# A recurrent mixer reordered: gates between the halves of the output branch, sigmoids by tanh, POOL for squares and a series, the first weight tile in quarters

## The chip, the cores and the metric

One core of one Trainium2 chip runs the whole program in one launch. The metric is the device time in microseconds (us): the median of three runs was 1516.95 (1516.81 to 1517.58). The engines are named as in the profile: PE (matmuls, with PEld for its weight loads), DVE (vector), ACT (scalar functions), POOL (GpSimd) and SP (issues DMAs).

## The reference, cut to what matters

Four layers on x of 256 tokens by 1024 features, in float32. Each layer is a norm, a mixer, a residual sum, a norm, an MLP with squared ReLU and a residual sum. The mixers are a recurrent one (RG-LRU), a sparse attention, RWKV-7 and a differential attention. Only the first mixer, and what leads up to it, is changed:

```python
def _rmsnorm(x, g):
    return x * lax.rsqrt(jnp.mean(x * x, axis=-1, keepdims=True) + RMS_EPS) * g

def _rglru_mixer(h, w_in, conv_w, conv_b, w_a, b_a, w_x, b_x, lam, w_out):
    proj = h @ w_in                                   # 1024 x 2048
    y = jax.nn.gelu(proj[..., :D_RNN], approximate=True)
    xb = _causal_depthwise_conv(proj[..., D_RNN:], conv_w, conv_b)   # 4 taps
    xr = xb.reshape(B, S, RG_BLOCKS, RG_BLOCK_W)      # 4 blocks of 256
    r = jax.nn.sigmoid(jnp.einsum('bsnc,ncd->bsnd', xr, w_a).reshape(B, S, D_RNN) + b_a)
    i = jax.nn.sigmoid(jnp.einsum('bsnc,ncd->bsnd', xr, w_x).reshape(B, S, D_RNN) + b_x)
    log_a = -RG_C * r * jax.nn.softplus(-lam)         # RG_C = 8
    a = jnp.exp(log_a)
    u = jnp.sqrt(-jnp.expm1(2.0 * log_a)) * (i * xb)
    _, hs = lax.associative_scan(_lru_combine, (a, u), axis=1)
    return (hs * y) @ w_out
```

## The kernel before, in words

Everything stays in SBUF, features over the 128 partitions in 8 chunks of 256 tokens. The weights come in 96 tiles of 128 x 4096 floats (2 MB), in the order of `TILE_ORDER` (line 39), into a ring of three slots. SP issues the first DMAs at once (lines 386 to 394) and each later tile when PE is done with the tile three places before (`tile_done`, line 337).

A product is taken in three passes of reduced-width floats. So each weight tile is split in quarters of 1024 columns: ACT writes the high part (`split` in the scalar block, L1078), DVE the difference (`split` in the vector block, L1484), and PE multiplies high by high, high by low and low by high (`product`, L441 to L443). The activations are split in the same way. A projection (`project`, line 459) has four output chunks m, each of 8 k with 3 matmuls, 96 matmuls of 256 columns; two m fill one of the eight PSUM banks. It waits for each quarter only in its first m. The gate stage is 96 matmuls too, over four blocks, and waits for all four quarters of its tile before its first. The output projection (`project_out`) has two tiles of 96 matmuls with half tokens and 512 columns (L508 to L510).

The order on each engine is that of its block, written out by hand; a `wait_ge` on a semaphore holds all that stands behind it there. The banks are handed out in turn (`_turns`), and `open_bank` makes PE wait until what the bank held has been read.

The first mixer runs on PE as x0, tv (a small product for the last layer), x1, gates, y0, y1, o0, o1. ACT copies x0 and x1 out of PSUM (`conv_in`, L1170), DVE does the four taps of the convolution (one L1641 and three L1648 for each chunk), ACT and DVE split the result (`xc_high` L1174, `xc_low` L1655), ACT takes the sigmoids (L1196), then exp and tanh of the decay (L1203, L1204), DVE squares a and multiplies (L1673, L1675, and the input gate L1677), ACT takes the root (L1210), DVE multiplies (L1684) and scans (L1687), ACT takes the gelu of y (L1215, L1220), and h times y is formed and split (`hy` L1695, `values_high` L1157, `values_low` L1598). The softplus of lam is a series on 128 x 8 values on DVE (L1608 to L1636). In the first norm ACT squares (L1091) and takes the root (L1095), DVE applies it (L1527), PE transposes (L456), ACT and DVE split (L1101, L1540). POOL in this stretch only fetches rows of norm factors and stores tv; from 128 us on it does 16 multiplications for the second mixer (L2133).

Of the kernel before, what the change touches and what calls it, by code (L numbers as in the profile page):

```python
# [7 lines left out]
P = 128  # L8
D = 1024
# [25 lines left out]
def _mlp_tiles(layer):  # L35
# [4 lines left out]
    ["rg_x0", "rg_x1", "rg_gates", "rg_y0", "rg_y1", "rg_o0", "rg_o1"] + _mlp_tiles(0)  # L40
# [19 lines left out]
PARAM_COLS = [("conv_w", 32), ("conv_b", 8), ("b_a", 8), ("b_x", 8), ("lam", 8),  # L60
# [68 lines left out]
for _n, _w in [("rg_x0", 2), ("tv", 1), ("rg_x1", 2), ("rg_gates", 8), ("rg_y", 4)]:  # L129
    _turns(_n, _w)  # L130
# [31 lines left out]
for _u in range(12):  # L162
# [6 lines left out]
    if _u >= 5 and _u % 2 == 1:  # L169
# [5 lines left out]
TURN_OF = {"rg_x0": ("rg_x0", 1), "rg_x1": ("rg_x1", 1), "rg_gates": ("rg_gates", 7), "rg_y0": ("rg_y", 1),  # L175
# [9 lines left out]
def build(nc, weights, params, consts, rows, heads, t5, x_in, out):  # L185
# [8 lines left out]
    with ctx:  # L194
# [60 lines left out]
        SM_NLAM, SM_GSUB, SM_LAM, SM_BGATE, SM_SP = 560, 562, 564, 566, 568  # L255

# [125 lines left out]
        def _(sp):  # L382
# [3 lines left out]
            for th in range(2):  # L386
                sp.dma_start(x[:, th, :], x_in[:, th, :]).then_inc(x_loaded[th], 16)
            sp.dma_start(scales[:, 0, :], bass.AP(rows.tensor, 0, [[0, P], [1, D]])).then_inc(sig("first_row_in"), 16)
            sp.dma_start(con[:, :], consts).then_inc(sig("consts_in"), 16)
            load(0)  # L390
            sp.dma_start(par[:, :], params).then_inc(params_in, 16)
            load(1)
            sp.dma_start(t5_onehot, t5).then_inc(sig("t5_in"), 16)
            load(2)
            for n in range(RING, NTILES):
                tile_done(sp, TILE_ORDER[n - RING])
                load(n)
# [8 lines left out]
        def _(pe):  # L406
# [12 lines left out]
            def whole_tile(name):  # L419

                n = TILE_AT[name]
                pe.wait_ge(slot_full[n % RING], 16 * (n // RING + 1))
# [36 lines left out]
            def project(name, q, src, ready=None, warm=0, beside=None):  # L459

                w_hi, w_lo = split_tile(name)
                for m in range(4):
# [127 lines left out]
            pe.wait_ge(sig("consts_in"), 16)  # L590
            norm(0, 0)
            norm(0, 1)
            project("rg_x0", TURN["rg_x0"], act_split, lambda k: acts_in(0, k), warm=8)
# [7 lines left out]
            w_hi, w_lo = split_tile("rg_gates")  # L601
            for quarter in range(4):
                quarter_in("rg_gates", quarter)
            for blk in range(4):
                pe.wait_ge(sig("xc_split"), blk + 1)
                for g in range(2):
                    q = TURN["rg_gates"] + 2 * blk + g
                    open_bank(q)
                    for m in range(2):
# [450 lines left out]
        def _(act):  # L1060
# [42 lines left out]
            def norm(i, next_tile=None):  # L1103
# [10 lines left out]
                if i == 0:  # L1114
                    for th in range(2):
                        for n in range(2):
                            square(i, th, n)
# [1200 lines left out]
```

## Time and profile before

| | us |
|---|---|
| median of three runs | 1516.95 |
| profiled execution, its own time | 1518.57 |
| its span, first to last instruction | 1516.8 |
| PE busy | 1409.6 (93%) |
| DVE busy | 913.9 (60%) |
| ACT busy | 675.4 (45%) |
| POOL busy | 72.0 (5%) |
| mean granted TensorE clock | 0.972 |

The span is shared by four layers, and the stretch that the change touches is its first 130 us. What counts there is when PE may start the next product. The busy spans of matmuls overlap (each is modelled to its end), so the pace of PE is read from their start times.

### The profile page before, as it was taken

The numbers are of one execution on the slowest core, as the hardware profiler recorded it, in microseconds if no ns is written. First come the engines' busy times: TensorE is split into PE (matmuls) and PEld (weight loads), VectorE is DVE, ScalarE is ACT, GpSimd is POOL, SyncE is SP. The second block draws the span as 40 slices with busy tenths as digits, with TensorE's granted clock in tenths as the row PEclk, the third lists the DMA queues.
The fourth block names the chain that finished last, engine by engine and source line by source line (L and its number), as shares of the span: only waits on it lengthen the run. The fifth ranks groups of instructions, "written<-read, shape, count | busy, mean of one in ns | idle before, by whom it ended". The sixth has DMA issues, their size and how long they took to land.

```text
span 1516.8 us, 26931 instructions
## 1 busy us (share of the span) xinstructions
PE 1409.6 (93%) x11772; PEld 1233.9 (81%) x11782; DVE 913.9 (60%) x1448; ACT 675.4 (45%) x1145; POOL 72.0 (5%) x69
## 2 busy tenths in 40 slices
PE   6889999999789999999997987999999997899997
PEld 5877999988657899987897985799997974599996
DVE  6686555671485556555966434765557459855556
ACT  5844544552363445441821222354444445354452
POOL 0004000000141000000001310000000000000000
PEclk9989999999889999999999999999999999999999
DMA  7334554552301555453150000455545440245451
GB/s 306 138 123 155 197 192 175 207 183 87 142 1 56 182 189 200 167 192 130 67 189 37 4 3 30 158 190 177 212 167 190 173 166 1 102 160 210 167 195 55
DMA packets 16917, 215.17 MB, mean 142 GB/s; under 512 B 1896, under 2 KB 1936, under 8 KB 3872
## 3 DMA queue, kind: packets, MB, share of 16 engines
q1 hardware_dynamic: 15168, 205.51, 37.0%
q0 software_dynamic: 1632, 7.94, 1.5%
q8 instruction: 93, 1.52, 0.4%
q14 instruction: 24, 0.20, 0.0%
HBM read 212.38 MB, written 1.06 MB: 141 GB/s over the span
## 4 chain that ended last, share of the span: by engine, by line
PE 76%; DVE 16%; ACT 4%; issue 2%; DMA 1%; POOL 0%; SPq 0%; DVEq 0%
PE psum L561 21%; PE psum L441 11%; PE psum L442 11%; PE psum L443 11%; PE psum L862 5%; DVE w_low L1484 5%; PE psum L962 2%; PE psum L508 2%; PE psum L491 2%; PE psum L510 2%; PE psum L509 2%; ACT w_high L1078 2%; PE psum L456 1%; PE psum L417 1%; DVE x L1531 1%
## 5 line engine op out<-in xcount | busy, mean ns | idle before, releaser
L1484 DVE TENSOR_TENSOR w_low<-ring,w_high 128x1024 fp32r<-128x1024 f32 x368 | 437.2, 1227 | 251.7 <-ACT w_high L1078 251.7
L1078 ACT ACTIVATE w_high<-ring 128x1024 fp32r<-128x1024 f32 x368 | 368.0, 1046 | 173.3 <-PE psum L561 154.6
L441 PE MATMUL psum<-act_split,w_high 128*128 128x256 f32 x1472 | 425.0, 289 | 3.6 <-DVE w_low L1484 3.5
L442 PE MATMUL psum<-act_split,w_high 128*128 128x256 f32 x1472 | 418.3, 284 | 0.0
L443 PE MATMUL psum<-act_split,w_low 128*128 128x256 f32 x1472 | 418.0, 284 | 0.0
L441 PEld LDWEIGHTS psum<-act_split,w_high 128*128 128x128 f32 x1472 | 284.0, 193 | 9.7 <-issue 4.4
L561 PE MATMUL psum<-w_high,up_split 128*128 128x512 f32 x1024 | 287.3, 391 | 0.8 <-DVE up_split L1587 0.8
L442 PEld LDWEIGHTS psum<-act_split,w_high 128*128 128x128 f32 x1472 | 284.3, 193 | 1.3
L443 PEld LDWEIGHTS psum<-act_split,w_low 128*128 128x128 f32 x1472 | 284.2, 193 | 0.0
L561 PEld LDWEIGHTS psum<-w_high,up_split 128*128 128x128 f32 x1024 | 191.0, 189 | 40.4 <-issue 2.4
L561 PE MATMUL psum<-w_low,up_split 128*128 128x512 f32 x512 | 163.5, 390 | 0.0
L561 PEld LDWEIGHTS psum<-w_low,up_split 128*128 128x128 f32 x512 | 96.4, 188 | 19.9
L1146 ACT ACTIVATE work<-psum 128x256 f32<-128x256 f32 x128 | 49.2, 385 | 109.0 <-PE psum L443 109.0
L1587 DVE TENSOR_TENSOR up_split<-work,up_split 128x256 fp32r<-128x256 f32 x128 | 54.6, 427 | 61.9 <-ACT up_split L1148 61.9
L1148 ACT ACTIVATE up_split<-work 128x256 fp32r<-128x256 f32 x128 | 53.5, 418 | 86.2 <-DVE work L1584 86.2
L862 PE MATMUL psum<-work 64*64 64x64 f32 (+1 forms) x2176 | 72.2, 227 | 9.3 <-POOL work L2157 8.4
L862 PEld LDWEIGHTS psum<-work 64*64 64x64 f32 x2176 | 71.8, 137 | 9.5 <-POOL work L2157 8.5
L1584 DVE TENSOR_TENSOR work<-work 128x256 f32<-128x256 f32 x128 | 54.5, 425 | 32.4 <-ACT work L1146 32.4
L508 PE MATMUL psum<-w_high,act_split 128*128 128x512 f32 x144 | 59.8, 415 | 6.2 <-DVE act_split L1598 5.6
L509 PE MATMUL psum<-w_low,act_split 128*128 128x512 f32 x144 | 57.7, 401 | 0.0
L510 PE MATMUL psum<-w_high,act_split 128*128 128x512 f32 x144 | 57.7, 400 | 0.0
L417 PE MATMUL psum<-zeros 128*128 128x512 bf16 x182 | 45.9, 398 | 1.1 <-issue 0.7
(293 smaller groups left out, 1455.3 us busy)
## 6 DMA issues: line engine op xcount, KB each, us to landing
ring<-weights SPq DMA_DIRECT2D x96, 2048.0 KB, 8.1
work<-rows POOLq DMA_DIRECT2D x4, 1024.0 KB, 6.5
work<-rows POOLq DMA_DIRECT2D x4, 512.0 KB, 5.7
con<-consts SPq DMA_DIRECT2D x1, 1088.0 KB, 8.7
x<-x_in SPq DMA_DIRECT2D x2, 512.0 KB, 4.5
work<-t_bias POOLq DMA_DIRECT2D x1, 1024.0 KB, 10.1
out<-x SPq DMA_DIRECT2D x4, 256.0 KB, 2.0
work<-rows SPq DMA_DIRECT2D x1, 512.0 KB, 6.1
```

The costliest lines, as they stand in the source:

```text
L417: mm(bank(q), zeros[:, :], view(zeros[:, 0:1], [[0, 512]]), start=True, stop=True)
L441: mm(out, w_hi, x_hi, start=start, stop=False)
L442: mm(out, w_hi, x_lo, start=False, stop=False)
L443: return mm(out, w_lo, x_hi, start=False, stop=stop)
L508: mm(bank(q), src[:, k, 0, t], w_hi[:, f], start=(k == 0), stop=False)
L509: mm(bank(q), src[:, k, 0, t], w_lo[:, f], start=False, stop=False)
L510: last = mm(bank(q), src[:, k, 1, t], w_hi[:, f], start=False, stop=(k == NC - 1))
L561: last = mm(bank(acc[(th, n)]), up_split[:, m, a, P * th:P * th + P], w[:, f], start=start and i == 0, stop=stop and i == len(pairs) - 1, ...
L862: last = mm(psum[half(hf), BANK[q], at:at + width], lhsT, rhs, start=True, stop=True)
L1078: A(high[:, HIGH_SLOT[name], f], ring[:, n % RING, f], ACT.Copy).then_inc(weights_high, 1)
L1484: V.tensor_tensor(low[:, n % RING, f], ring[:, n % RING, f], high[:, HIGH_SLOT[name], f].bitcast(f32), ALU.subtract).then_inc(weights_spli ...
L1587: V.tensor_tensor(up_split[:, m, 1, :], up_sq[:, m, :], up_split[:, m, 0, :].bitcast(f32), ALU.subtract).then_inc(sig("up_split"), 1)
```

## The change

Seven things change, all before the first MLP.

1. SP's order is x half 0, lam alone (4 KB), the norm row, the identity alone (64 KB), x half 1, the first weight tile in four DMAs, the other parameters, tile 1, t5, tile 2, and last the other constants. ACT waits for each quarter of tile 0 by itself. PE waits for the identity, not for all constants, and runs 8 matmuls of zeros before its first transposes and 6, not 8, before x0.
2. The series for softplus begins before the first norm (DVE forms |lam|, ACT its exp, DVE a ratio) and is finished on POOL. DVE does no small steps between the splits any more.
3. The first norm on ACT squares three quarters of x, takes the first root, squares the last, takes the second root, and mixes the splits of the first tile with the copies of the transposes; DVE does the like.
4. ACT does the first tap of the convolution with the bias (Identity with scale and bias from PSUM), so a chunk has three taps on DVE. The split of x1 stands behind the first `conv_in` and `conv`.
5. The tile order is x0, x1, y0, gates, y1. PE does the first half of y0, gate blocks 0 and 1, the second half of y0, gate blocks 2 and 3, y1. y of y0 is copied to SBUF, its gelu comes later. The banks are handed out in this order.
6. sigmoid(z) is formed as (1 + tanh(z/2))/2: the halves and ones are folded into the decay's scale and bias and into the root's scale of 0.25. The decay is done for each pair of gate blocks as soon as it is there.
7. POOL adds the one to the input gate, squares a and multiplies the input gate by the convolution's result; DVE keeps only `decay_square`. The split of o0 is in two halves on both engines.

```diff
-for _n, _w in [("rg_x0", 2), ("tv", 1), ("rg_x1", 2), ("rg_gates", 8), ("rg_y", 4)]:
+for _n, _w in [("rg_x0", 2), ("tv", 1), ("rg_x1", 2), (("rg_y", 0), 1), (("rg_gates", 0), 4), (("rg_y", 1), 1),
+               (("rg_gates", 1), 4), (("rg_y", 2), 1), (("rg_y", 3), 1)]:
     _turns(_n, _w)
...
+            project("rg_y0", TURN[("rg_y", 0)], act_split, ms=(0, 1))
+            gate_blocks(0)
+            project("rg_y0", TURN[("rg_y", 1)] - 1, act_split, ms=(2, 3))
+            gate_blocks(1)
+            project("rg_y1", TURN[("rg_y", 2)], act_split)
...
 (scalar block)
-                    for th in range(2):
-                        for n in range(2):
-                            square(i, th, n)
+                    for th, n in ((0, 0), (0, 1), (1, 0)):
+                        square(i, th, n)
                     root(i, 0)
+                    square(i, 1, 1)
+                    root(i, 1)
+                    split(next_tile, [0])
                     out(0)
-                    root(i, 1)
+                    split(next_tile, [1])
                     out(1)
+                    split(next_tile, [2, 3])
...
             conv_in(0)
+            split("rg_x1")
             conv_in(1)
             (tv)
             xc_high(0)
-            split("rg_gates")
+            split("rg_y0")
             xc_high(1)
             conv_in(2)
             xc_high(2)
             conv_in(3)
-            split("rg_y0")
+            split("rg_gates")
             xc_high(3)
...
+            def decay(i):
+                for blk in (2 * i, 2 * i + 1):
+                    (two gates, two m: filled, ACT.Tanh scale=0.5 bias=half bias)
+                settle()
+                for c in range(4 * i, 4 * i + 4):
+                    (ACT.Exp and ACT.Tanh with scale and bias per partition)
+                done(ins, "rg_decay")
+            output_branch(0)
+            decay(0)
+            output_branch(1)
             split("rg_y1")
+            decay(1)
             for i in range(2):
                 act.wait_ge(sig("rg_sq"), i + 1)
-                done(A(u, u, ACT.Sqrt), "rg_root")
+                done(A(u, u, ACT.Sqrt, scale=0.25), "rg_root")
-            split("rg_o0")
-            (gelu of y 0, 1, 2 from PSUM)
+            split("rg_o0", [0, 1])
+            (gelu of y 0, 1 in SBUF)
             values_high 0, 1
-            (gelu of y 3)
+            (gelu of y 2, 3 from PSUM)
+            split("rg_o0", [2, 3])
             values_high 2, 3
...
 (vector block)
             conv(0)
+            split("rg_x1")
             conv(1)
             xc_low(0)
-            split("rg_gates")
+            split("rg_y0")
             xc_low(1)
             conv(2)
             xc_low(2)
             conv(3)
-            split("rg_y0", range(2))
+            split("rg_gates")
             xc_low(3)
+            decay_square(0)
+            split("rg_y1")
+            decay_square(1)
             for i in range(2):
+                dve.wait_ge(sig("rg_gated"), i + 1)
                 dve.wait_ge(sig("rg_root"), i + 1)
                 (multiply, four scans)
+                if i == 0:
+                    split("rg_o0", [0, 1])
...
             hy(0)
             hy(1)
-            split("rg_o0")
             hy_low(0)
             hy(2)
             hy_low(1)
             hy(3)
+            split("rg_o0", [2, 3])
             hy_low(2)
...
 (POOL, behind the series of 21 steps on 128 x 8 values, the row fetch and the store of tv)
+            for i in range(2):
+                for blk in range(2):
+                    read_out(pool, TURN[("rg_gates", i)] + 2 * blk + 1)
+                step(G.tensor_scalar(buf(RG_I)[:, s], buf(RG_I)[:, s], 1.0, None, ALU.add))
+                pool.wait_ge(sig("rg_decay"), i + 1)
+                done(G.tensor_tensor(buf(RG_R)[:, s], buf(RG_A)[:, s], buf(RG_A)[:, s], ALU.mult), "rg_a2")
+                done(G.tensor_tensor(buf(RG_I)[:, s], buf(RG_I)[:, s], buf(RG_XC)[:, s], ALU.mult), "rg_gated")
```

## Rows read from the trace of the kernel before

**Rows 1.** The page: shares of the chain that ended last, by engine

```profile
PE 76%; DVE 16%; ACT 4%; issue 2%; DMA 1%; POOL 0%; SPq 0%; DVEq 0%
```

**Rows 2.** Stages: window, engines' busy us (x instructions), PE clock, DMA share, GB/s

```profile
90.00:100.00 10.00, 3.45 (x8) 2.80 (x9) 9.65 (x13) 4.11 (x7) 0.00 (x0) 0.70 0.57 210
```

**Rows 3.** Timeline of PE: start, us, instruction, [idle before <- releaser]

```profile
22.64 0.39 PE L441 MATMUL psum<-act_split,w_high 128*128 128x256 f32 x1 [0.16 <-DVE w_low L1484]
...
32.92 0.39 PE L441 MATMUL psum<-act_split,w_high 128*128 128x256 f32 x1
...
44.42 0.28 PE L443 MATMUL psum<-act_split,w_low 128*128 128x256 f32 x1
...
56.85 0.58 PE L441 MATMUL psum<-xc_split,w_high 128*128 128x256 f32 x1 [2.49 <-DVE xc_split L1655]
...
59.98 0.28 PE L443 MATMUL psum<-xc_split,w_low 128*128 128x256 f32 x1
...
75.83 0.36 PE L441 MATMUL psum<-act_split,w_high 128*128 128x256 f32 x1 [2.98 <-DVE w_low L1484]
...
96.55 0.76 PE L508 MATMUL psum<-w_high,xc_split 128*128 128x512 f32 x1 [7.14 <-DVE xc_split L1598]
```

**Rows 4.** The page, DMA issues: tile, count, KB each, us from issue to landing

```profile
ring<-weights SPq DMA_DIRECT2D x96, 2048.0 KB, 8.1
...
con<-consts SPq DMA_DIRECT2D x1, 1088.0 KB, 8.7
x<-x_in SPq DMA_DIRECT2D x2, 512.0 KB, 4.5
...
work<-rows SPq DMA_DIRECT2D x1, 512.0 KB, 6.1
```

**Rows 5.** Timeline of ACT, first 90 us

```profile
7.40 1.28 ACT L1095 ACT_TABLE_LOAD   x1
...
16.87 3.89 ACT L1078 ACTIVATE w_high<-ring 128x1024 fp32r<-128x1024 f32 x4
...
55.91 5.22 ACT L1196 ACTIVATE work<-psum,par 128x256 f32<-128x256 f32 x14
...
67.46 0.51 ACT L1203 ACTIVATE work<-work,small 128x256 f32<-128x256 f32 x1
...
87.68 1.57 ACT L1215 ACTIVATE work<-psum 128x512 f32<-128x512 f32 x3
```

**Rows 6.** Timeline of DVE, first 100 us

```profile
17.95 4.63 DVE L1484 TENSOR_TENSOR w_low<-ring,w_high 128x1024 fp32r<-128x1024 f32 x4 [0.25 <-ACT w_high L1078]
...
28.64 0.17 DVE L1616 TENSOR_SCALAR small<-small 128x8 f32<-128x8 f32 x1
...
33.11 0.73 DVE L1641 TENSOR_SCALAR work<-work,par 128x256 f32<-128x256 f32 x2
33.88 2.71 DVE L1648 SCALAR_TENSOR_TENSOR work<-work,par 128x256 f32<-128x256 f32 x6
...
70.80 1.23 DVE L1673 TENSOR_TENSOR work<-work 128x1024 f32<-128x1024 f32 x1 [11.73 <-ACT work L1204]
...
83.91 2.44 DVE L1687 TENSOR_TENSOR_SCAN work<-work 128x256 f32<-128x256 f32 x4
...
89.97 1.29 DVE L1695 TENSOR_TENSOR work<-work 128x512 f32<-128x512 f32 x2
```

**Rows 7.** POOL's two large operations, by line: duration ns min/median/max, first and last start

```profile
L2157 POOL TENSOR_TENSOR work<-work,con x5: 4490/4536/4538, 830.1 to 873.9; 128x2048 f32<-128x2048 f32 x5
...
L2133 POOL TENSOR_SCALAR work<-con x16: 847/852/1293, 128.2 to 143.6; 128x256 f32<-128x256 f32 x16
```

**Rows 8.** Timeline of DVE beside POOL's L2133, and after it

```profile
140.61 1.23 DVE L1484 TENSOR_TENSOR w_low<-ring,w_high 128x1024 fp32r<-128x1024 f32 x1 [0.50 <-ACT w_high L1078]
141.77 0.61 DVE L1584 TENSOR_TENSOR work<-work 128x256 f32<-128x256 f32 x1
...
157.71 0.42 DVE L1584 TENSOR_TENSOR work<-work 128x256 f32<-128x256 f32 x1
```

More of the change, by code:

```diff
@@ L457, in norm, with project @@
                     last.then_inc(bank_filled, 1)
-            def project(name, q, src, ready=None, warm=0, beside=None):
+            def project(name, q, src, ready=None, warm=0, beside=None, ms=range(4)):
                 w_hi, w_lo = split_tile(name)
-                for m in range(4):
+                for m in ms:
                     if m % 2 == 0:
@@ L1169, in conv_in @@
                 filled(q)
-                taken(A(rg_xp[:, 2 * i:2 * i + 2, 3:3 + T], bank2(q), ACT.Copy), q)
+                A(rg_xp[:, 2 * i:2 * i + 2, 3:3 + T], bank2(q), ACT.Copy)
+                for m in range(2):
+                    c = 2 * i + m
+                    ins = A(chunks(RG_XC)[:, c, :], bank2(q)[:, m, :], ACT.Identity, scale=col("conv_w", 24 + c),
+                            bias=col("conv_b", c))
+                taken(ins, q)
             def xc_high(i):
@@ L1198, in _, with output_branch @@
-            settle()
-            split("rg_y1")
-            act.wait_ge(sig("sp_done"), 1)
-            for i in range(2):
-                for c in range(4 * i, 4 * i + 4):
-                    A(chunks(RG_A)[:, c, :], chunks(RG_R)[:, c, :], ACT.Exp, scale=small[:, SM_SP + 16 + c:SM_SP + 17 + c])
-                    ins = A(chunks(RG_U)[:, c, :], chunks(RG_R)[:, c, :], ACT.Tanh,
-                            scale=small[:, SM_SP + 8 + c:SM_SP + 9 + c])
-                done(ins, "rg_decay")
+            def output_branch(i):
+                q = TURN[("rg_y", i)]
+                filled(q)
+                taken(A(chunks(RG_Y)[:, 2 * i:2 * i + 2, :], bank2(q), ACT.Copy), q)
@@ L1553, in norm @@
                             acts_low(i, th, n)
+                        split(next_tile, [th])
+                    split(next_tile, [2, 3])
                     return
@@ L1601, in _ @@
             done(V.memset(rg_xp[:, :, 0:3], 0.0), "conv_padded")
[L1602 to L1607 removed]
+            dve.wait_ge(sig("lam_in"), 16)
+            sp, s1, s2, s4 = (small[:, SM_SP + 8 * i:SM_SP + 8 * i + 8] for i in (0, 3, 4, 6))
             step(V.tensor_scalar(s4, col("lam", 0, 8), -1.0, None, ALU.mult))
@@ L1610, in _ @@
             done(V.tensor_tensor(sp, col("lam", 0, 8), s4, ALU.max), "sp_abs")
-            lam = view(col("da_lam"), [[2, 2]])[0:64, :]
-            done(V.tensor_tensor(small[0:64, SM_LAM:SM_LAM + 2], lam, view(col("da_lam", 1), [[2, 2]])[0:64, :],
-                                 ALU.mult), "lam_prod")
-            split("rg_x1")
             dve.wait_ge(sig("sp_exp"), 1)
```

197 lines of the change are left out of this document (105 added, 92 removed), and 2 rows, old and new, of the table TURN_OF.

## The prediction

> **What bounds the kernel now.** I read the chain of waits first. Over the whole span it lies on PE for 76% [rows 1], and from 130 us on nothing of the change is met, so all that can move is the time at which PE gets through the first mixer. Then I read the timeline of PE up to there, for its starts and for who released it. It works with hardly a gap from the end of the first projection's quarter waits until some 54 us; then it waits 2.5 us for DVE, 3.0 us for DVE's split of y1, and 7.1 us for DVE's first split product before the output projection starts at 96.55 [rows 3]. Behind such gaps the granted clock is at its lower level of 1.2 GHz for some 3 to 4 us: starts lie 0.21 us apart from 56.85 to 59.98, where a projection without a gap has 96 matmuls between 32.92 and 44.54, 0.12 apart [rows 3]; in the window of the largest gap PE is busy 3.45 of 10 us at a clock of 0.70 [rows 2]. DVE is busy 9.65 us in that same window: ahead of the output projection DVE is the bound, and it is fed by ACT. The mark by which I judge the change is therefore one time: when does the first matmul of the output projection start. After it both kernels do the same work in the same order on each engine, but for two quarter splits of o0.
>
> **The change part by part**, as a new timetable. Durations used: a tile split 3.9 us on ACT (0.97 a quarter) [rows 5] and 4.6 on DVE (1.14 a quarter) [rows 6]; half a projection or half of the gates 5.8 us (48 at 0.12) [rows 3]; a pair of conv chunks with three taps 2.7 [rows 6]; a 128 x 512 operation 0.6 on DVE [rows 6] and 0.55 on ACT [rows 5]; 0.05 to 0.1 for a signal.
>
> *Start.* Before, x arrives (4.5 us from issue), then the row (6.1, so at 7.75), then the constants (8.7, so at 10.8) [rows 4], and ACT loads the root's table at 7.40 [rows 5], when all four squares are done. Now x half 1 is behind the row, lam and the identity: 1.5 MB and a little lie before its end, as they did before the row's end, so it lands at 7.75 plus 0.2 to 0.9 for 256 short packets that no row shows; I take 8.3. The third square must wait for it and stands ahead of the root, so the table load moves from 7.40 to 9.0. This is a loss of 1.6. Root at 10.4, DVE's first half of the norm to 11.9, second root at 12.4. PE need not wait for the constants, but this hides behind the norm: the transposes would start at 11.2 instead of 10.9. The gain comes after: ACT splits quarter 0 from 12.4, DVE has the four low activation parts (2.4) and four quarters (4.6) behind each other from 14.1, so quarter 3 is ready at 21.1. Before, PE had it at 22.64 [rows 3]. Gain 1.5. The four quarter DMAs bring nothing by themselves: 2 MB ends near 13.5 by the rate of the constants, and quarters 2 and 3 are wanted from 16.6. Exp of lam ahead of the squares costs ACT 0.2 us while it would wait for x half 1 anyway.
>
> *To the gates.* PE's x0 has its first two m at 24.8, all at 30.5. ACT: copy and two first taps (3 x 0.45) to 26.1; no instruction of this kind is in the trace, the sigmoids from PSUM of the same shape take 5.22/14 = 0.37 [rows 5], and 0.8 for the two is what DVE paid for its own (0.73) [rows 6], so the bounds are 0 and 0.2 off. From there DVE is one chain: conv 0 to 28.9, split x1 to 33.5, conv 1 to 36.2, low part 36.8, split y0 to 41.3, low part 41.9, conv 2 to 44.6; then ACT's high part and `conv_in(3)`, which stands behind it, to 46.5; conv 3 to 49.2, split of the gates to 53.8. What is removed from DVE here is the series (28.64 to 33.11) and four first taps of 0.73 [rows 6], 7.4 us. Most of this is not earned: DVE and ACT now stand idle for 5 us from 21.1 to 26.1, since the split of x1 was moved behind `conv_in(0)`. PE: x1 waits for its quarter 3 until 33.5 and ends at 42.9; first half of y0 to 48.7; then a **new gap of 5.1 us**, as the gate blocks want all quarters of a tile that DVE now splits last. It is twice the gap at 56.85, so I charge the lower clock: 14 to 17 starts at 0.21, that is 1.3 to 1.6 us. Gates 0 and 1 end at 61.2, second half of y0 at 67.0.
>
> *Decay.* ACT has the tanh of blocks 0 and 1 and the eight exp and tanh (3.3 us: from 67.46 to DVE's release at 70.80 [rows 5, 6]) done at 65.7, and waits for y0 (67.0). Copy to 67.6, split y1 to 71.5, eight tanh (3.0) to 74.6, eight exp and tanh to 78.0. Now POOL: its addition of one has from 74.6 to 78.0. Of this kind there is only 128x256 at 0.85 [rows 7]; with 1024 columns it lies between 0.85 and 3.4, so it is hidden or late by 0.1. The square of a: the two-input operation with 2048 columns takes 4.5 [rows 7], half of that is 2.3, against 1.23 on DVE [rows 6]: to 80.4. DVE's `decay_square` to 81.6; ACT's root of half 0 is done by then. DVE: multiply and scans of half 0 (3.65 [rows 6]) to 85.3, two quarters of o0 to 87.6, half 1 to 91.2, two products h times y (1.29 [rows 6]) to 92.5. The low part of the first would release PE at 93.2. But the output projection's first bank is bank 0, which y's last quarter holds, and its gelu stands on ACT behind two high parts and the gelu before it (0.55 each): 94.3. Before, the release came from DVE [rows 3], so that gelu was in time. POOL's second product runs beside DVE's next two operations. Beside L2133 a two-input operation of DVE took 0.61 instead of 0.42, and POOL's own up to 1.29 instead of 0.85 [rows 7, 8]; but DVE's 128x1024 difference in the same window kept its 1.23 [rows 8]. So 0 to 1.1 us for the two; I take 0.3. **PE starts at 94.6 instead of 96.55.**
>
> *Behind it.* DVE splits the last quarters of o0 to 98.1 and the last two low parts to 99.3; PE, at the lower clock, wants them at 98.7 and 99.9. No stall. y1 ends on PE at 84.4, and the tiles behind it land 8.1 us [rows 4] after their slots are free, all ahead of their splits. The small steps on POOL (21, between 0.1 and 0.6 us each by the smallest and the shortest rows of POOL, not more than 15 us) end by 25 and are wanted at 51.
>
> The ScalarE: Activation LUTs page of the Trainium skill (Table sets) says that cheap functions are in every set and that exp and tanh share one, so the new order needs no load for the first taps. This case's trace agrees for exp beside tanh; Identity is in no run yet. The skill's GPSIMD Engine Reference (4.1, Engine selection) speaks against the change: it would keep element-wise products on VectorE, being about twice as slow on GpSimd. The row agrees (2.3 against 1.23), and this is the 1.1 us of the chain that the move itself costs in half 1.
>
> **Sum.** Against the profiled span of 1516.8: 94.6 - 96.55 = -2.0, so a span of 1514.8 and, with the 1.8 that its own time of 1518.57 has around the span, 1516.6 for that execution. The profiled execution was 1.6 above the median; from the median of 1516.95 the forecast is **1515.0**.
>
> **Rivals.** (A) The timetable above, 1515.0; its own range is 1513.9 to 1516.0. (B) *Every cheap end holds*: x half 1 lands with the old row's time (-0.5), POOL doesn't disturb DVE (-0.3), the lower clock lasts 14 starts (-0.2), first taps at 0.37 (-0.2): 94.6 falls to 93.4, time 1513.8. For it: each is a row's own value. Against: all must hold together. (C) *The first projection at the lower clock.* PE is nearly idle from 16 to 21 us, 24 matmuls in pieces between quarters, where before it came from eight matmuls of zeros right before. If the clock falls there, the next 24 to 30 matmuls cost 0.09 each more, 2.2 to 2.7 us less what overlaps the waits: about 1.5 at `conv_in(0)`, from which all follows: 1516.5. For it: a gap of 2.5 us was enough at 56.85. Against: no single gap here is over 1.2 us. (D) *POOL becomes the bound*, the slower side. The additions take 3.4 and, beside DVE, 1.5 times that [rows 7]: POOL is then 2 us late with the square of half 1, the square itself takes 3.4 (1.1 more), and DVE's two operations pay the full 1.1; the late and disturbed chain adds 4.3 to A: 1519.3. It decides as soon as the addition of half 1 ends later than 78.0. Against: DVE is idle while the additions run. The Trainium skill's GPSIMD Engine Reference (1, Specifications) says that GpSimd's SBUF interface is shared with VectorE when that has two SBUF inputs; this is the mechanism of D, and the trace agrees by the 0.61 against 0.42.
>
> **How the numbers follow.** A 0.50, B 0.22, C 0.18, D 0.10. What a measurement can tell from no change is about 0.2%, 3.0 us: faster is below 1513.9, slower above 1520.0. Faster takes most of B and a little of A, 0.23; slower half of D and what I have not seen, 0.07; the rest is 0.70. The range 1513.0 to 1517.9 leaves out one in ten below (B with more) and one above (most of D).
>
> **What would show it.** Right: the table load at about 9, the last quarter of x0 at about 21.1, a gap on PE from 48.7 to 53.8 with a lower clock after it, POOL's square of half 1 near 78 to 80.4 and about 2.3 long, the first L508 near 94.6 with its release by ACT's gelu and not by DVE. Wrong: a start of the output projection outside 93.4 to 96, an ACT chain that waits for POOL's series, or a difference that arises behind 130 us.

## The result, and the profile after

| | before | after |
|---|---|---|
| median, us | 1517.03 (1515.37 to 1518.97, 14 runs) | 1519.91 (1518.38 to 1522.28, 14 runs) |
| span of the profiled execution, us | 1516.8 | 1516.9 |
| its own time, us | 1518.57 | 1518.65 |
| first matmul of the output projection, us | 96.55 | 98.94 |

The ratio after/before is 1.002, its 95% interval 1.0013 to 1.0027. The changed kernel is 2.9 us slower where 2.0 less was forecast; it lies outside the range, and on the other side. The forecast's own mark, the start of the output projection, was to come at 94.6 and comes at 98.94.

The page of the kernel after answers to [rows 1] with its fourth part, and to [rows 4] with a line of its sixth:

```profile
PE 74%; DVE 18%; ACT 5%; issue 2%; DMA 1%; POOL 0%; SPq 0%; DVEq 0%; ACTq 0%; POOLq 0%
...
x<-x_in SPq DMA_DIRECT2D x2, 512.0 KB, 5.9
```

The stage of [rows 2] and the one behind it (window, busy us of each engine with its instructions, granted clock, DMA share, GB/s): PE now does 3 matmuls in this window instead of 8, at the same low clock.

```profile
90.00:100.00 10.00, 1.06 (x3) 0.87 (x4) 9.44 (x14) 5.21 (x9) 0.00 (x0) 0.68 0.58 210
98.00:108.00 10.00, 9.06 (x30) 7.27 (x31) 9.60 (x12) 7.61 (x10) 0.00 (x0) 0.71 0.00 0
```

PE's timeline of the kernel after (start, us, instruction, idle before and releaser), for [rows 3]. 22.64 has become 23.07, the gap before the gates 5.28 us, and the last gap 9.64 us with ACT's gelu as its releaser:

```profile
23.07 0.39 PE L449 MATMUL psum<-act_split,w_high 128*128 128x256 f32 x1 [0.16 <-DVE w_low L1526]
...
56.57 0.55 PE L449 MATMUL psum<-xc_split,w_high 128*128 128x256 f32 x1 [5.28 <-DVE w_low L1526]
...
98.94 0.80 PE L516 MATMUL psum<-w_high,xc_split 128*128 128x512 f32 x1 [9.64 <-ACT work L1261]
```

ACT's timeline, for [rows 5]. The third square waits for x half 1 until 10.26, the table load comes at 11.00 (7.40 before), and the eight exp and tanh of half 1 stand 0.49 us apart:

```profile
10.26 0.63 ACT L1109 ACTIVATE work<-x 128x512 f32<-128x512 f32 x1 [3.44 <-DMA x<-x_in]
...
11.00 1.28 ACT L1113 ACT_TABLE_LOAD   x1
...
27.55 1.01 ACT L1193 ACTIVATE work<-psum,par 128x256 f32<-128x256 f32 x2
...
69.59 0.60 ACT L1221 ACTIVATE work<-psum 128x512 f32<-128x512 f32 x1 [0.83 <-PE psum L451]
70.08 3.89 ACT L1096 ACTIVATE w_high<-ring 128x1024 fp32r<-128x1024 f32 x4
73.88 3.02 ACT L1231 ACTIVATE work<-psum,small 128x256 f32<-128x256 f32 x8
76.93 0.60 ACT L1237 ACTIVATE work<-work,small 128x256 f32<-128x256 f32 x1
77.44 0.58 ACT L1238 ACTIVATE work<-work,small 128x256 f32<-128x256 f32 x1
...
80.39 0.59 ACT L1238 ACTIVATE work<-work,small 128x256 f32<-128x256 f32 x1
80.99 1.28 ACT L1251 ACT_TABLE_LOAD   x1
```

DVE's timeline, for [rows 6]. `decay_square` is L1698: it took 1.22 and 1.23 in the kernel before (L1675) and takes 3.41 here, both times.

```profile
51.59 4.62 DVE L1526 TENSOR_TENSOR w_low<-ring,w_high 128x1024 fp32r<-128x1024 f32 x4
...
70.84 3.41 DVE L1698 SCALAR_TENSOR_TENSOR work<-work 128x1024 f32<-128x1024 f32 x1 [14.03 <-POOL work L2188]
74.17 5.46 DVE L1526 TENSOR_TENSOR w_low<-ring,w_high 128x1024 fp32r<-128x1024 f32 x4
83.05 3.41 DVE L1698 SCALAR_TENSOR_TENSOR work<-work 128x1024 f32<-128x1024 f32 x1 [3.42 <-POOL work L2188]
86.38 1.21 DVE L1708 TENSOR_TENSOR work<-work 128x1024 f32<-128x1024 f32 x1
...
95.96 1.29 DVE L1724 TENSOR_TENSOR work<-work 128x512 f32<-128x512 f32 x2
97.34 0.69 DVE L1642 TENSOR_TENSOR xc_split<-work,xc_split 128x512 fp32r<-128x512 f32 x1
```

POOL did no arithmetic in this stretch before. Its product (L2189) starts at 70.77 and 82.97, 0.07 and 0.08 us ahead of DVE's L1698; the experiments show that this is the cause:

```profile
64.94 2.78 POOL L2186 TENSOR_SCALAR work<-work 128x1024 f32<-128x1024 f32 x1 [29.49 <-ACT work L1231]
68.91 1.90 POOL L2188 TENSOR_TENSOR work<-work 128x1024 f32<-128x1024 f32 x1 [1.18 <-ACT work L1238]
70.77 2.40 POOL L2189 TENSOR_TENSOR work<-work 128x1024 f32<-128x1024 f32 x1
77.04 3.26 POOL L2186 TENSOR_SCALAR work<-work 128x1024 f32<-128x1024 f32 x1 [3.87 <-issue]
81.12 1.90 POOL L2188 TENSOR_TENSOR work<-work 128x1024 f32<-128x1024 f32 x1 [0.82 <-ACT work L1238]
82.97 2.40 POOL L2189 TENSOR_TENSOR work<-work 128x1024 f32<-128x1024 f32 x1
```

**Why the two spans are equal and the medians are not.** Two table loads of ACT frame one stretch of the second mixer. The first lies at 399.74 before and 402.41 after: the 2.4 us of the mark are still there (+2.67). The second lies at 486.95 before and 486.15 after: the profiled execution of the kernel before lost 3.5 us in this stretch (87.2 against 83.7). Windows of the kernel before, then of the one after (columns as above):

```profile
402.00:442.00 40.00, 26.93 (x176) 19.57 (x174) 31.90 (x128) 25.59 (x102) 14.12 (x18) 0.74 0.10 41
442.00:487.00 45.00, 42.17 (x285) 31.38 (x284) 31.07 (x75) 20.85 (x55) 12.31 (x15) 0.96 0.13 48
```

```profile
402.00:442.00 40.00, 27.23 (x198) 20.53 (x196) 31.85 (x135) 27.15 (x104) 14.84 (x18) 0.79 0.15 53
442.00:487.00 45.00, 41.69 (x290) 30.73 (x286) 32.16 (x78) 22.25 (x57) 11.63 (x15) 1.00 0.13 48
```

The granted clock is 0.74 and 0.96 in the one, 0.79 and 1.00 in the other. No work of the change lies there, and other executions fall on either side: 83.7 to 83.8 us in e1, e4 and e6, 85.0 to 86.2 in e8, e7 and e5, 87.3 in e2. So one span does not compare two of these kernels. Below, mechanisms are read by the mark, and times by medians with their intervals.

### The profile page after: what moved, and what is told of

It reads as the page before. It is cut to its first block, busy times and chain, and to the rows that moved or that the text cites. A ratio compares the mean times of both kernels' runs of the same rounds, so it can differ in the third digit from the quotient of the medians.

```text
span 1516.9 us, 26963 instructions
## 1 busy us (share of the span) xinstructions
PE 1407.5 (93%) x11778; PEld 1229.2 (81%) x11788; DVE 907.4 (60%) x1418; ACT 678.5 (45%) x1153; POOL 91.6 (6%) x96
## 4 chain that ended last, share of the span: by engine, by line
PE 74%; DVE 18%; ACT 5%; issue 2%; DMA 1%; POOL 0%; SPq 0%; DVEq 0%; ACTq 0%; POOLq 0%
PE psum L569 21%; PE psum L449 11%; PE psum L451 10%; PE psum L450 10%; PE psum L878 5%; DVE w_low L1526 5%; PE psum L978 2%; PE psum L516 2%; PE psum L499 2%; PE psum L517 2%; PE psum L518 2%; ACT w_high L1096 1%; PE psum L425 1%; ACT work L1326 1%; PE psum L464 1%
## 5 line engine op out<-in xcount | busy, mean ns | idle before, releaser
L425 PE MATMUL psum<-zeros 128*128 128x512 bf16 x188 | 49.1, 408 | 9.1 <-DMA con<-consts 8.0
```

The costliest lines, as they stand in the source:

```text
L425: mm(bank(q), zeros[:, :], view(zeros[:, 0:1], [[0, 512]]), start=True, stop=True)
```

## The experiments

All marks are the start of the output projection's first matmul; "from y" is the distance to it from ACT's copy of y's second half (L1221), 69.59 to 98.94 = 29.35 us in the kernel after. It takes two things out that differ between executions of this order: when x half 1 lands, and the clock behind the gap before the gates (from 56 to 62 us the granted clock was 0.72 in the kernel after, 0.62 in e2 and 0.50 in e7). Each mark is of one profiled execution.

**e1_x_early.** x half 1 is sent where the kernel before had it.

```diff
             sp.dma_start(x[:, 0, :], x_in[:, 0, :]).then_inc(x_loaded[0], 16)
+            sp.dma_start(x[:, 1, :], x_in[:, 1, :]).then_inc(x_loaded[1], 16)
             sp.dma_start(par[:, 0:lam_at], ...
...
-            sp.dma_start(x[:, 1, :], x_in[:, 1, :]).then_inc(x_loaded[1], 16)
```

> The changed kernel with one edit: x half 1 is sent right behind x half 0, ahead of lam, the norm row and the identity. In the changed kernel x half 1 was released at 10.26 us, where 8.3 had been forecast, and in the kernel before at 6.05. Theory 1, the transfers issued behind it share the engines with it: it lands near 6.1, the third square follows the second at about 6.7, the table load is at 7.5 instead of 11.0, and the chain then waits for the norm row (7.7) and not for x. The first matmul of the output projection comes 2 to 3.3 us earlier than 98.9. Rival, the small packets of lam (32 bytes each) hold everything behind them whatever the order: lam lands at 5.5 or later, the row at 8.5 or later, and the gain is under 1 us. Time against the kernel before: +0.0 to +1.0 us by the first, +2 by the second.

Measured: 1517.86 us (11 runs), ratio to before 1.0001 (0.9992 to 1.001); mark 96.60, 2.34 earlier than after. ACT's timeline of e1 has no wait in the squares, and the root's load at 8.56 instead of 11.00:

```profile
7.84 0.61 ACT L1109 ACTIVATE work<-x 128x512 f32<-128x512 f32 x1
...
8.56 1.28 ACT L1113 ACT_TABLE_LOAD   x1
```

L1698 still takes 3.42 and 3.40. So the 2.4 us by which the load comes earlier come out at the mark (2.3), and the order of these transfers is worth as much as the whole loss: with it put right the changed kernel stands level with before. The load did not come at 7.5, as I expected: lam now lands later, its exp is the first work of ACT, and the first square starts at 6.61 instead of 5.50.

**e11_lam_behind.** Only lam's transfer (4 KB, in 32-byte pieces) moves, behind x half 1.

```diff
-            sp.dma_start(par[:, 0:lam_at], ...).then_inc(sig("lam_in"), 16)
...
             sp.dma_start(x[:, 1, :], x_in[:, 1, :]).then_inc(x_loaded[1], 16)
+            sp.dma_start(par[:, 0:lam_at], ...).then_inc(sig("lam_in"), 16)
```

> The changed kernel with the 4 KB of lam sent behind x half 1 and not ahead of the norm row. Theory, the 128 packets of 32 bytes hold the row and x half 1 behind them: x half 1 is released at about 9.1 or earlier, not at the 9.1 to 10.6 seen so far. Rival, what is issued behind x half 1 (the first weight tile in four transfers) shares the engines with it: no change, 9.6 to 10.6. The exp of lam is the first instruction of ACT, so all of ACT waits for it in both cases, and lam then lands at 6 us or later; the output projection starts no earlier than 97.

Measured in one execution: 1518.57 us, mark 99.23. x half 1 landed 6.3 us after its issue at 2.1, so at 8.4; in the kernel after it took 7.7 from 2.6, and in the seven profiled executions of that order the third square, which waits for it, started at 9.1 to 10.6. But lam now landed 5.9 after 2.6, its exp stands ahead of the squares on ACT, and the load came at 11.06. This agrees with lam's short pieces holding up the larger transfer, and doesn't show it. Why x half 1 takes 7.7 us there stays open.

**e2_gated_dve.** The product with the input gate goes to DVE; the addition and the square stay on POOL.

```diff
+                dve.wait_ge(sig("rg_plus"), i + 1)
+                done(V.tensor_tensor(buf(RG_I)[:, s], buf(RG_I)[:, s], buf(RG_XC)[:, s], ALU.mult), "rg_gated")
...
-                step(G.tensor_scalar(buf(RG_I)[:, s], buf(RG_I)[:, s], 1.0, None, ALU.add))
+                done(G.tensor_scalar(buf(RG_I)[:, s], buf(RG_I)[:, s], 1.0, None, ALU.add), "rg_plus")
...
-                done(G.tensor_tensor(buf(RG_I)[:, s], buf(RG_I)[:, s], buf(RG_XC)[:, s], ALU.mult), "rg_gated")
```

> The changed kernel with one edit: the product of the input gate and the convolution goes from POOL back to DVE, ahead of DVE's wait for the square of a; POOL keeps the additions and the squares. In the changed kernel decay_square took 3.41 us on DVE both times, beside POOL's product of 2.40; before it took 1.23. Theory 1, POOL's two-input product keeps DVE's two-input operation waiting: both decay_squares take 1.2, and the start of the output projection moves from 98.9 to about 96.7, as the product of half 1 fits into DVE's idle time before the square. Rival, the operation is slow by itself in this kernel (its operands were just written by another engine): it stays at 3.4 and the start moves later by up to 1.2. Time against the kernel before: about +0.5 by the first, +3 to +4 by the second.

Measured: 1518.52 us (11 runs), ratio 1.0001 (0.9992 to 1.001); mark 97.14, from y 27.10, 2.25 less. DVE's timeline of e2: the product costs 1.23 while DVE waits anyway, and `decay_square` is back at its old price.

```profile
80.31 1.23 DVE L1698 TENSOR_TENSOR work<-work 128x1024 f32<-128x1024 f32 x1 [3.32 <-POOL work L2188]
83.44 1.23 DVE L1700 SCALAR_TENSOR_TENSOR work<-work 128x1024 f32<-128x1024 f32 x1 [1.90 <-POOL work L2190]
```

**e5_before_gated_pool.** The kernel before with this product alone on POOL, so that contention stands by itself.

```diff
-                step(V.tensor_tensor(buf(RG_I)[:, s], buf(RG_I)[:, s], buf(RG_XC)[:, s], ALU.mult))
-                settle()
+                dve.wait_ge(sig("rg_gated"), i + 1)
...
+                nc.gpsimd.tensor_tensor(buf(RG_I)[:, s], buf(RG_I)[:, s], buf(RG_XC)[:, s],
+                                        ALU.mult).then_inc(sig("rg_gated"), 1)
```

> The kernel before with one part of the change alone: the product of the input gate (L1677) goes from DVE to POOL, released by the decay like DVE's square (L1673). So POOL's two-input product starts together with a tensor_tensor of DVE, with a scalar_tensor_tensor behind it. Theory 1, whoever of the two starts first holds the other until it is done: one of the first two DVE operations of each half takes 3.3 to 3.5 and the other its own 1.23, so DVE is later with the squares by 2.2 a half and saves 1.23 of the product: the output projection starts 0 to 1.5 us later than 96.55. Rival, only the scalar_tensor_tensor is slow beside POOL: L1673 keeps 1.23 whenever it overlaps POOL, and L1675 is stretched. Second rival, both share the rate: both DVE operations are stretched, by 1 each.

Measured: 1519.34 us (10 runs), ratio 1.001 (1.0001 to 1.002); mark 98.64, 2.1 later than before (0.25 of it from the start, where the transposes begin at 11.12 instead of 10.87), more than the most I expected. DVE's and POOL's timelines of e5:

```profile
71.19 1.23 DVE L1673 TENSOR_TENSOR work<-work 128x1024 f32<-128x1024 f32 x1 [11.88 <-ACT work L1204]
72.45 3.27 DVE L1675 SCALAR_TENSOR_TENSOR work<-work 128x1024 f32<-128x1024 f32 x1
75.65 6.77 DVE L1484 TENSOR_TENSOR w_low<-ring,w_high 128x1024 fp32r<-128x1024 f32 x4
```

```profile
71.31 6.63 POOL L2133 TENSOR_TENSOR work<-work 128x1024 f32<-128x1024 f32 x2 [36.69 <-ACT work L1204]
```

Whoever starts first keeps its own time, and the other waits for its end: DVE's square started 0.12 ahead and took 1.23, POOL's product waited for it (3.34 us where it takes 2.40 in the kernel after), and the next operation of DVE then waited for POOL (3.27 instead of 1.22). It is not a rate shared between two. Here DVE paid twice: POOL's second product came ahead of the split of y1, whose four quarters took 6.77 instead of 4.63. That is 4.2 us of waiting for the two products of 1.22 that DVE no longer does.

**e12_pool_late.** POOL's product waits until DVE's `decay_square` is done.

```diff
+                pool.wait_ge(sig("rg_sq"), i + 1)
                 done(G.tensor_tensor(buf(RG_I)[:, s], buf(RG_I)[:, s], buf(RG_XC)[:, s], ALU.mult), "rg_gated")
```

> The changed kernel with one wait more: POOL's product of each half waits for DVE's decay_square of that half. If POOL and DVE exclude each other by whole instructions when both read two tensors from SBUF, decay_square takes 1.2 both times, and the wait of 2.2 us appears at the next DVE instruction that starts behind POOL's product: a quarter of the split of y1 for half 0, one of the four scans for half 1 (the multiplication starts ahead of POOL). The output projection starts within 0.5 us of where it did, measured from ACT's second copy of y (29.35 us). Rival, only scalar_tensor_tensor in place is slow beside POOL: no other instruction is longer than before, and the start comes 2.2 us earlier.

Measured in one execution: 1519.58 us, mark 99.70, from y 29.27: nothing gained. DVE's timeline of e12: L1698 has 1.23 again, and what it saves is paid by the split of y1 (7.67 instead of 5.46) and by the scans (4.54 instead of 2.44).

```profile
72.82 7.67 DVE L1526 TENSOR_TENSOR w_low<-ring,w_high 128x1024 fp32r<-128x1024 f32 x4
83.89 1.23 DVE L1698 SCALAR_TENSOR_TENSOR work<-work 128x1024 f32<-128x1024 f32 x1 [3.39 <-POOL work L2188]
...
86.28 4.54 DVE L1711 TENSOR_TENSOR_SCAN work<-work 128x256 f32<-128x256 f32 x4
```

The wait moved to the two-input work that DVE had at that time; with DVE never idle behind `decay_square`, this place was not free either.

**e7_no_pool.** All three on DVE, the addition and the product in one instruction.

```diff
+                done(V.scalar_tensor_tensor(buf(RG_I)[:, s], buf(RG_I)[:, s], 1.0, buf(RG_XC)[:, s],
+                                            ALU.add, ALU.mult), "rg_gated")
+                dve.wait_ge(sig("rg_decay"), i + 1)
+                done(V.tensor_tensor(buf(RG_R)[:, s], buf(RG_A)[:, s], buf(RG_A)[:, s], ALU.mult), "rg_a2")
...
-            (POOL's three operations of each half)
```

> The changed kernel without POOL in the mixer: DVE forms (i+1) times the convolution in one scalar_tensor_tensor in its idle time ahead of each decay, then squares a itself (1.23 instead of POOL's 1.90), then decay_square. If POOL's part costs by its own slower square and by holding DVE off, the start of the output projection falls from 98.94 by 2.2 (the wait) and 0.6 (the square): 96.1 to 96.4, 0.8 to 1.0 earlier than with the product alone moved back. Rival, the three operations on DVE make it late: no earlier than 97.1.

Measured: 1518.99 us (10 runs), ratio 1.001 (1.0 to 1.002); mark 96.83, from y 26.45, 2.90 less. (By the mark alone it is 2.1 less: x half 1 had landed 0.6 earlier, and the lower clock behind the gap before the gates lasted longer, so y's second half was copied at 70.38 instead of 69.59.) DVE's timeline of e7: from exp's last result to the end of `decay_square` 2.5 us pass, where POOL and DVE need 5.4 (80.99 to 86.38).

```profile
77.78 1.23 DVE L1700 SCALAR_TENSOR_TENSOR work<-work 128x1024 f32<-128x1024 f32 x1 [1.17 <-issue]
81.80 1.23 DVE L1703 TENSOR_TENSOR work<-work 128x1024 f32<-128x1024 f32 x1 [2.80 <-ACT work L1238]
83.06 1.22 DVE L1705 SCALAR_TENSOR_TENSOR work<-work 128x1024 f32<-128x1024 f32 x1
```

**e4_split_first.** On ACT and DVE the split of x1 stands ahead of `conv_in(0)` and `conv(0)`.

```diff
-            conv_in(0)
             split("rg_x1")
+            conv_in(0)
...
-            conv(0)
             split("rg_x1")
+            conv(0)
```

> The changed kernel with one edit: on ACT and DVE the split of x1 stands ahead of the first copy and convolution again, as in the kernel before, in the 5 to 7 us in which both engines sat idle (DVE 23.2 to 28.6). If the order was what threw the removed DVE work away, the chain from 28.6 loses 4.5 us of split but must wait for PE's second half of x0 (32.7): conv 0 ends at 31.4 as before, conv 1 at 36.8, split of the gates ends 1.5 to 2 us earlier than 56.2, and the output projection starts 1.5 to 2 us earlier than 98.9. Rival, the stall after the gates' first half is refilled elsewhere (ACT's chain of tanh and exp sets the pace): under 0.5 us.

Measured: 1517.55 us (10 runs), ratio 1.0 (0.9991 to 1.0009); mark 97.71, 1.23 earlier, with x half 1 at the same time (10.25 against 10.26). The split of the gates ends at 54.7 instead of 56.2. The 5 us in which DVE stood idle before `conv_in(0)` return only in part: `conv(1)` now waits 3.04 us for ACT's first taps, which wait for PE.

**e8_gelu_first.** The two last gelus ahead of the two high parts of h times y.

```diff
-            values_high(xc_split, xc_raw, 0, "hy_raw", "hy_high")
-            values_high(xc_split, xc_raw, 1, "hy_raw", "hy_high")
             for i in (2, 3):
...
+            values_high(xc_split, xc_raw, 0, "hy_raw", "hy_high")
+            values_high(xc_split, xc_raw, 1, "hy_raw", "hy_high")
```

> The changed kernel with one edit on ACT: the gelu of y's last two quarters stands ahead of the two high parts of h times y, in the time in which ACT waits for DVE (91.9 to 96.7). The last gelu holds bank 0, which the output projection opens first. By the trace PE started at 98.94, 0.03 after that gelu (98.90), where the first low part was there at 98.03. Theory: PE starts at 98.1, 0.8 earlier. Rival, the bank is not what held it: no change.

Measured: mark 97.09, of which x half 1 had landed 1.15 us earlier by chance; from y 28.59, 0.76 less. The releaser is DVE again (PE's timeline of e8), so ACT's gelu did end the last wait, for under 1 us:

```profile
97.09 0.77 PE L516 MATMUL psum<-w_high,xc_split 128*128 128x512 f32 x1 [8.88 <-DVE xc_split L1642]
```

The time did not follow: 1520.66 us (10 runs), ratio 1.0015 (1.0006 to 1.0025), where the kernel after has 1.002 (1.0013 to 1.0027). A difference of under 1 us can't be told from these times.

**e6_gates_whole.** The kernel after with the halves undone: gates, y0, y1 as tiles and on PE, both halves of the decay ahead of y1's split on ACT and DVE, gelu from PSUM.

```diff
-    ["rg_x0", "rg_x1", "rg_y0", "rg_gates", "rg_y1", "rg_o0", "rg_o1"] + _mlp_tiles(0)
+    ["rg_x0", "rg_x1", "rg_gates", "rg_y0", "rg_y1", "rg_o0", "rg_o1"] + _mlp_tiles(0)
...
-            output_branch(0)
             decay(0)
-            output_branch(1)
-            split("rg_y1")
             decay(1)
+            split("rg_y1")
```

> The changed kernel with the named part undone: tile order x0, x1, gates, y0, y1, all four gate blocks ahead of y0, splits of y0 and gates swapped back on ACT and DVE, decay of half 0 and half 1 one behind the other ahead of the split of y1, gelu from PSUM for all of y. POOL keeps its operations. Theory, the order costs: PE needs no gates split at 56.2, as it has 11.5 us of y0 to do after the gates; the last block waits for the fourth low part (about 57), so a gap of 3 us stays, but the decay is done by 70 instead of 81 and the path to the output projection is then PE's y1, which ends at 85 to 86.5. The first matmul of the output projection comes at 87 to 90 instead of 98.9, so 8 us less in all against the changed kernel and 5 to 7 less than the kernel before. Rival, the order is neutral (the sum of DVE's work sets the end, wherever it lies): 96 to 99.

Measured: 1511.95 us (5 runs), ratio 0.9961 (0.9949 to 0.9974); mark 91.89, 7.05 earlier than after, with L1698 still at 3.41 and 3.35. PE's timeline of e6: the gap before the gates falls from 5.28 to 2.69 us, and the last from 9.64 to 0.69. Part of it only moves: PE now waits 4.89 us for DVE's split of y1 (at 76.72), where the kernel after waits 1.00.

```profile
57.17 0.39 PE L449 MATMUL psum<-xc_split,w_high 128*128 128x256 f32 x1 [2.69 <-DVE xc_split L1678]
...
91.89 0.50 PE L516 MATMUL psum<-w_high,xc_split 128*128 128x512 f32 x1 [0.69 <-ACT work L1253]
```

**e10_before_decay_first.** In the kernel before, only the split of y1 moves behind both halves of the decay, on ACT and on DVE.

```diff
-            split("rg_y1")
...
+            split("rg_y1")
...
-                if i == 0:
-                    split("rg_y1")
+            split("rg_y1")
```

> The kernel before with one edit: the split of y1 stands behind both halves of the decay on ACT and DVE, not between the sigmoids and the decay. In the run with whole gates the path to the output projection was no longer the decay. Theory, it is this place of the split that held the kernel before, not tanh, POOL or the halves: decays end 4 us earlier (70 instead of 74), the split of y1 costs PE nothing or up to 2 us more at 72.9 (its first quarter is wanted there), DVE's two squares no longer have 4.6 us of split between them, and the output projection starts at 90 to 93 instead of 96.55: ratio 0.997. Rival, PE's y1 is late by the whole split (first quarter at 76 or later) and then sets the end: 95 to 97, ratio 1.000.

Measured: 1510.99 us (5 runs), ratio 0.9961 (0.9947 to 0.9974); mark 92.47 against 96.55, 4.1 earlier, of which some 0.25 from the start (the transposes begin at 10.61 instead of 10.87). In e10's timelines of DVE and PE the decay's six operations stand behind each other at 66.71 to 73.99, PE's wait for y1 is 2.69 us, no longer than the 2.98 of [rows 3]:

```profile
66.71 1.23 DVE L1673 TENSOR_TENSOR work<-work 128x1024 f32<-128x1024 f32 x1 [7.90 <-ACT work L1203]
...
74.02 4.63 DVE L1484 TENSOR_TENSOR w_low<-ring,w_high 128x1024 fp32r<-128x1024 f32 x4
```

```profile
75.39 0.36 PE L441 MATMUL psum<-act_split,w_high 128*128 128x256 f32 x1 [2.69 <-DVE w_low L1484]
...
92.47 0.47 PE L508 MATMUL psum<-w_high,xc_split 128*128 128x512 f32 x1 [3.34 <-DVE xc_split L1598]
...
93.24 0.40 PE L508 MATMUL psum<-w_high,xc_split 128*128 128x512 f32 x1
```

The time gains 6.0 us, 2 more than the mark, and the clock of the output projection accounts for it. In the kernel before, the same instruction behind the gap of 7.14 us takes 0.63, not 0.40 (PE's timeline of before):

```profile
97.97 0.63 PE L508 MATMUL psum<-w_high,xc_split 128*128 128x512 f32 x1
```

In the first 5 us behind the mark the granted clock was 0.57 in the kernel before and 1.00 in e10, and ACT's next table load (for the root of the next norm) came 21.67 us behind the mark in the one (118.22) and 19.63 in the other (112.10): 6.1 us earlier in all, which is about the gain in time.

**e9_combined.** What the runs pointed to, together: the edits of e1, e4, e6 and e7, nothing else.

> All that is found so far in one kernel: gates whole ahead of y0, x half 1 right behind x half 0, POOL's three operations on DVE, the split of x1 ahead of the first convolution. Theory: x0 is ready 2.4 us earlier than in the changed kernel, so PE ends y1 at 82 to 84 and the output projection starts at 84 to 86.5, 10 to 12 us earlier than the kernel before (96.55); time 0.993 of the kernel before. Rival, the gains overlap: the last gate block still waits for DVE's fourth low part behind the split of y0, and y1's tile or split is late; 88 to 91, ratio 0.996.

Measured: 1505.37 us (1503.18 to 1505.82, 5 runs), ratio to before 0.9917 (0.9905 to 0.993): 12 us less than before, and 14.5 less than the median of the kernel after. PE's timeline of e9: of the three gaps of [rows 3] 1.59 us are left before the gates, 0.89 before y1 and 2.06 before the output projection, and the mark is at 84.31, 12.2 us earlier than before.

```profile
53.77 0.39 PE L449 MATMUL psum<-xc_split,w_high 128*128 128x256 f32 x1 [1.59 <-DVE xc_split L1678]
...
84.31 0.47 PE L516 MATMUL psum<-w_high,xc_split 128*128 128x512 f32 x1 [2.06 <-DVE xc_split L1641]
```

## Why the prediction was wrong, step by step

What bounds the kernel was read rightly: only the start of the output projection moves, and the median moved with it (+2.4 at the mark, +2.9 in the time). Also right were the shape of the timetable, the new gap before the gates (5.1 forecast, 5.28 measured) with the lower clock behind it, the gelu of bank 0 as last releaser, no table load between the new neighbours on ACT, and nothing late behind the mark. The forecast failed by 4.3 us at the mark, in three terms of the sum that were each taken too small:

| step | forecast, us | measured, us | off |
|---|---|---|---|
| x half 1 lands | 8.3 | 10.26 | +2.0 |
| split of the gates ready | 53.8 | 56.2 | +2.4, of which 2.0 from x (contained in the next row) |
| y0's second half copied | 67.6 | 70.1 | +2.5 |
| eight exp and tanh of half 1 | 3.3 | 4.0 | +0.7 |
| POOL's square | 2.3 | 1.90 | -0.4 |
| `decay_square` with contention | 1.2 + 0.3 for two | 3.41 | +1.9 |
| output projection starts | 94.6 | 98.94 | +4.3 |

**First: x half 1 lands with 0.2 to 0.9 for lam.** Bytes ahead of it were counted, and the count gave 8.3; across executions it lands at 9.1 to 10.6. The bound was taken from a row of another transfer (the row of the norm, 6.1 us), and nothing in the trace of before held a short-packet transfer in front of a large one. The table load was forecast to lose 1.6, and the new order behind it to win that back and 1.5 more (last quarter of x0 at 21.1 against 22.64). The load lost 3.6, and the last quarter came at 23.07. e1 shows it: with the old order alone the change costs nothing against before.

**Second: contention between 0 and 1.1 us, taken at 0.3.** This is rival D's mechanism with its price mis-sized, and what it hinged on was put wrongly: D was to start once POOL's addition was late. It was not late (it ended at 80.30, ahead of ACT's exp and tanh at 80.99, in spite of its 3.26), and yet `decay_square` waited out nearly the whole of POOL's product, 2.2 us of 2.40. That the median of 1519.9 lies close to D's 1519.3 is luck: D added it up from a late addition and a square of 3.4 us, and neither came. The bound came from a pair of small operations (0.61 against 0.42 [rows 8]), read as a slowdown by half. Read by the later runs it may have been a short wait for the rest of a short instruction; that row by itself doesn't tell. For two-input products of 2.4 us the wait is nearly as long as they are: e5, e12 and e2 show it. The Trainium skill states this on a page that the prediction did not draw on, SBUF — State Buffer (Who interferes with whom): a VectorE instruction with two SBUF inputs and a GpSimd instruction that reads SBUF exclude each other for a whole instruction, and the one that starts first wins. The trace agrees, by 3.41 against 1.23 here and by the order of starts in e5. By that rule the product would have been priced at POOL's whole 2.4 us. For POOL's addition, which reads one tensor, the trace does not agree: DVE's split lost 0.8 us beside it (5.46 against 4.62), not the 2.8 that the addition takes.

**Third: exp and tanh at 0.40 each.** That pitch is of instructions with one scale taken from a tile; the new ones take scale and bias from tiles, and stand 0.49 apart. The Trainium skill's ScalarE: Activation LUTs page (What ACT_TABLE_LOAD costs) gives 93 ns for each such operand; 0.49 against 0.40 agrees with it.

The 0.4 us that POOL's square was cheaper came back, and so did some 0.4 in small overlaps of the steps on ACT and behind `decay_square`. The move to POOL was costed as a loss of 1.1 in half 1 and was one of 2.9 (e7). So the experiments price the parts, by the marks: the transfer order 2.3 (e1), POOL 2.9 (e7), the late split of x1 1.2 (e4), and 7.0 for e6, which undoes the halves and besides puts the split of y1 behind the decay. That place of the split is not of the change (the kernel before has the split ahead of the decay too): moved by itself in the kernel before it gives 4.1 (e10), so that about 3 are left for the halves, by subtraction across two kernels; no run has the halves alone undone. Together these are 13.4 us, and e9, which has all four edits, comes 14.6 before the kernel after. That the mark is only 2.4 later than before must then be paid by what the changed kernel gains elsewhere, such as seven microseconds of DVE work gone or on POOL before the gates and 6 table loads of ACT instead of 8 up to 131 us; no run takes these gains apart.

Rivals B and C did not come either. Of B's cheap ends x half 1 and POOL failed as above, and the first taps stand 0.45 us apart, as the timetable had them, not 0.37. C, the first projection at the lower clock, is ruled out by the trace: from 19 to 33 us the granted clock was 1.00 in both kernels.

What I did not see at all: the decay waits behind y1's split in both kernels, half 1 of it on ACT in the kernel after, both halves on ACT and half 1 again on DVE in the kernel before. e10 takes this away in the kernel before and gains 4.1 us at the mark by moving one call on each of two engines. In the kernel before, the chain of waits showed DVE as the releaser of the last gap, and I asked what DVE would save, not what stood ahead of its input.

## What to carry to other kernels

Before work goes from VectorE to GpSimd, look at what VectorE does in those microseconds: beside two-input work a large two-input POOL instruction added nearly its whole length to VectorE's chain here, and moving it later only moved the wait (e12). When a transfer is pushed back in a queue, ask which engine has it ahead of something that others wait for, and price it from executions, not from bytes. And at a large gap follow the releaser's own input back until an engine is found doing work that is not needed yet; here moving one such split (4.1 us at the mark, 6.0 in the time, e10) gained more than any other single edit.

## What the runs showed of the hardware that I had not expected

- A two-input product of POOL and two-input operations of DVE exclude each other by whole instructions. 1024-column DVE operations of 1.23 took 3.41 (after) and 3.27 (e5) beside a POOL product, four scans 4.54 instead of 2.44 (e12).
- POOL by form, 1024 columns of f32: the square of one tensor 1.90, the product of two 2.40, adding a constant 2.78. The one that reads one tensor and a constant is the slowest. Beside DVE's split it takes 3.26 and delays that by 0.8 (5.46 against 4.62), less than a whole instruction; why less is open.
- One and the same stretch of the second mixer takes 83.7 to 87.3 us at different granted clocks from execution to execution, more than the effect measured here.
- The same 512 KB transfer in fourth or fifth place landed 6.3 to 8.0 us after its issue, and 4.7 to 4.9 after it in second place (e1, e9, the kernel before).
- The length of a gap on PE did not say by itself which clock came behind it: 2.49 us before the gates of the kernel before were followed by a granted clock of 0.72 from 56 to 62 us, and 2.69 us at the same place in e6 by 1.00.
